# Sums of squares of the first attention: two passes of rounded halves in place of one 32-bit product

## The reference, cut to what matters

```python
def rmsnorm(x, g):
    xf = x.astype(jnp.float32)
    y = xf * lax.rsqrt(jnp.mean(xf * xf, axis=-1, keepdims=True) + EPS)
    return (y * g.astype(jnp.float32)).astype(x.dtype)
...
    k = jnp.concatenate([kv[..., :A_NOPE], jnp.broadcast_to(k_rope[:, :, None, :], (B, L, A_HEADS, A_ROPE))], axis=-1)
    return rmsnorm(k, k_g), kv[..., A_NOPE:]
...
    q = (rmsnorm(h[..., :A_Q_LORA], cq_g) @ w_uq).reshape(B, L, A_HEADS, A_QK)
    return rmsnorm(q, q_g)
```

## Time and profile before

| | |
|---|---|
| median of 3 runs | 3061.49 us (3056.06 to 3071.42) |
| profiled execution, its own time | 3064.81 us |
| span of its instructions | 3063.0 us |
| mean granted TensorE clock | 0.982 of full |
| TensorE busy | 2933.3 us (96%) |
| VectorE busy | 1799.2 us (59%) |
| ScalarE busy | 1360.8 us (44%) |
| GpSimd busy | 701.9 us (23%) |

### The profile page before, as it was taken

The page is one execution under the profiler, slowest core; times in us unless marked ns, Lnnn a source line. Parts: engine busy times, 40 slices in busy tenths (PEclk is TensorE's granted clock), DMA queues, the critical chain, the costliest instruction groups (busy, mean ns, idle before and its releaser), DMA issues. The chain is left out here.

```text
span 3063.0 us, 38159 instructions
## 1 busy us (share of the span) xinstructions
PE 2933.3 (96%) x14042; PEld 2109.6 (69%) x14042; DVE 1799.2 (59%) x2476; ACT 1360.8 (44%) x2162; POOL 701.9 (23%) x509
## 2 busy tenths in 40 slices
PE   5998999999999999999999999979999999999999
PEld 2563444444478888889998887844448788888887
DVE  5124656455535877789863444356643887777442
ACT  3014665656633544445653432136662544445231
POOL 0001555455520133330000000034550133331000
PEclk8998999999999999999999999989999999999999
DMA  9920000000020222224664431122211122224453
GB/s 372 369 98 2 4 3 3 4 2 2 7 110 35 77 83 83 83 83 159 210 196 125 145 102 49 41 66 66 64 45 49 63 78 85 84 85 146 137 171 100
DMA packets 101718, 282.14 MB, mean 92 GB/s; under 512 B 12129, under 2 KB 27745, under 8 KB 94562
## 3 DMA queue, kind: packets, MB, share of 16 engines
q1 hardware_dynamic: 101570, 280.16, 27.4%
HBM read 237.25 MB, written 27.26 MB: 86 GB/s over the span
## 5 line engine op out<-in xcount | busy, mean ns | idle before, releaser
L1367 ACT ACTIVATE z_wh<-part 128x512 fp32r<-128x512 f32 x266 | 166.5, 629 | 335.3 <-PE PS L1238 211.4
L1743 DVE TENSOR_TENSOR z_wdl<-part,z_wdh 128x512 fp32r<-128x512 f32 (+3 forms) x208 | 148.7, 721 | 255.5 <-ACT z_wdh L1420 255.2
L1236 PE MATMUL PS<-s_uh,z_wh 128*128 128x512 f32 x736 | 286.6, 389 | 0.0
L1238 PE MATMUL PS<-s_uh,z_wl 128*128 128x512 f32 x736 | 286.6, 389 | 0.0
L1237 PE MATMUL PS<-s_ul,z_wh 128*128 128x512 f32 x736 | 286.5, 389 | 0.0
L1420 ACT ACTIVATE z_wdh<-part 128x512 fp32r<-128x512 f32 (+3 forms) x208 | 135.2, 655 | 303.7 <-DMA part<-in_w_down 302.7
L1664 DVE TENSOR_TENSOR z_wl<-part,z_wh 128x512 fp32r<-128x512 f32 x266 | 218.2, 833 | 46.3 <-ACT z_wh L1367 46.3
L2400 POOL TENSOR_TENSOR X<-X 128x1024 f32<-128x1024 f32 x96 | 229.4, 2389 | 59.6 <-ACT X L2635 58.7
L1223 POOL TENSOR_TENSOR part<-part,part 128x512 f32<-128x512 f32 x38 | 56.8, 1495 | 777.1 <-DMA part<-in_w_up 777.1
L2635 ACT ACTIVATE X<-PS 128x512 f32<-128x512 f32 x252 | 145.9, 593 | 143.8 <-PE PS L2422 135.5
L2731 DVE TENSOR_REDUCE part<-PS 128x1 f32<-128x512 f32 (+1 forms) x312 | 161.9, 580 | 13.7 <-PE PS L2534 12.9
(11 more groups left out here) (412 smaller groups left out, 7594.6 us busy)
## 6 DMA issues: line engine op xcount, KB each, us to landing
part<-in_w_up SPq DMA_DIRECT2D x132, 512.0 KB, 3.3
part<-in_mod_w SPq DMA_DIRECT2D x48, 1024.0 KB, 7.2
part<-in_w_down SPq DMA_DIRECT2D x96, 256.0 KB, 2.7
gated<-part SPq DMA_DIRECT2D x44, 512.0 KB, 2.6
part<-gated SPq DMA_DIRECT2D x87, 256.0 KB, 5.5
part<-in_w_down SPq DMA_DIRECT2D x32, 384.0 KB, 3.1
part<-in_w_down SPq DMA_DIRECT2D x32, 320.0 KB, 3.2
part<-in_w_down SPq DMA_DIRECT2D x48, 192.0 KB, 2.4
```

What stands on the lines that cost most here:

```text
L1236: pe.matmul(bank_, w_h, x_h, start=start, stop=False, skip_group_check=further)
L1238: return pe.matmul(bank_, w_l, x_h, start=False, stop=stop, skip_group_check=further)
L1367: act.activation(wh[i][:, :], full[b][i], ACT.Copy).then_inc(s["hi"], 1)
L1743: dve.tensor_tensor(wdl[j][:, :width(e)], wd[j][:, :width(e)], wdh[j][:, :width(e)].bitcast(F32), ALU.subtract).then_inc(s["wdl"], 1)
```

## The change

The squares are split: ScalarE copies each square into a rounded high half (`skh` for keys, `sqh` for queries), VectorE subtracts it from the square, which gives the low half (`skl`, `sql`), and TensorE multiplies ones, held in the rounded type as `unity`, by the high half and by the low half, into the same sum in PSUM. The semaphore that `squares` waits for is now that of the subtraction. `square_low` stands in VectorE's queue after `turn` and ahead of the unit step of the chunk before. The shared rows 64 to 96 are split once, at the start. `sq` and `t1` trade their places in memory.

```diff
-            raw, sq = [[Xf[:, rest + (2 * x + n) * BANK:rest + (2 * x + n + 1) * BANK] for n in range(2)] for x in range(2)]
-            t1 = [take(BANK) for _ in range(2)]
+            raw, t1 = [[Xf[:, rest + (2 * x + n) * BANK:rest + (2 * x + n + 1) * BANK] for n in range(2)] for x in range(2)]
+            sql = [place(f"h0_sql{n}", o + n * BANK, BANK) for n in range(2)]
+            sq = [take(BANK) for _ in range(2)]
+            sqh = [place(f"h0_sqh{n}", 9088 + n * BANK, BANK) for n in range(2)]
...
                     def squares(p, w):
 
                         lo, hi = CH[w % 3]
-                        pe.wait_ge(s["sq"], 6 * p + w + 1)
+                        pe.wait_ge(s["sql"], 6 * p + w + 1)
                         if w == 4:
                             pe.wait_ge(s["out"], 6 * p + 4)
                         at_least(pe, "lo", 6 * p + w - 1)
-                        src = sk[0:A_QK, lo:hi] if w < 3 else sq[w % 2][0:A_QK, :hi - lo]
-                        pe.matmul(ps(NB[w % 2], hi - lo, slice(0, A_QK)), ones[0:A_QK, 0:A_QK], src,
-                                  start=True, stop=True).then_inc(s["nt"], 1)
+                        for x in (skh, skl) if w < 3 else (sqh[w % 2], sql[w % 2]):
+                            part = x[0:A_QK, lo:hi] if w < 3 else x[0:A_QK, :hi - lo]
+                            mm = pe.matmul(ps(NB[w % 2], hi - lo, slice(0, A_QK)), unity[0:A_QK, :], part,
+                                           start=x in (skh, sqh[w % 2]), stop=x in (skl, sql[w % 2]))
+                        mm.then_inc(s["nt"], 1)
...
                             act.activation(sk[0:64, lo:hi], ps(PB[w], n, slice(0, 64)), ACT.Square).then_inc(s["sq"], 1)
+                            act.wait_ge(s["sq"], 6 * p + w + 1)
+                            act.activation(skh[0:64, lo:hi], sk[0:64, lo:hi], ACT.Copy).then_inc(s["sqh"], 1)
...
                             act.activation(sq[w % 2][0:96, :n], ps(PB[w], n, slice(0, 96)), ACT.Square)\
                                 .then_inc(s["sq"], 1)
+                            act.wait_ge(s["sq"], 6 * p + w + 1)
+                            act.activation(sqh[w % 2][0:96, :n], sq[w % 2][0:96, :n], ACT.Copy).then_inc(s["sqh"], 1)
...
+                    act.activation(skh[64:96, :], sk[64:96, :], ACT.Copy).then_inc(s["kh0"], 1)
+                    act.activation(unity[:, :], ones[:, 0:A_QK], ACT.Copy).then_inc(s["kh0"], 1)
...
+                    def square_low(p, w):
+                        lo, hi = CH[w % 3]
+                        n = hi - lo
+                        dve.wait_ge(s["sqh"], 6 * p + w + 1)
+                        if w < 3:
+                            out_, in_, h_ = skl[0:64, lo:hi], sk[0:64, lo:hi], skh[0:64, lo:hi]
+                        else:
+                            out_, in_, h_ = [x[w % 2][0:96, :n] for x in (sql, sq, sqh)]
+                        dve.tensor_tensor(out_, in_, h_.bitcast(F32), ALU.subtract).then_inc(s["sql"], 1)
...
                         if kind == "prep" and 3 <= n < 5:
                             turn(p, n)
+                        if kind == "prep" and n < 6:
+                            square_low(p, n)
                         if kind == "prep" and 0 < n < 7:
                             unit(p, b, n - 1)
...
+                    dve.wait_ge(s["kh0"], 1)
+                    dve.tensor_tensor(skl[64:96, :], sk[64:96, :], skh[64:96, :].bitcast(F32), ALU.subtract).then_inc(s["kh0"], 1)
                     for n, x in enumerate((kh[1], kl[1], qh[1], ql[1])):
                         dve.memset(x[96:P, :].bitcast(F32), 0.0).then_inc(s["pad1"], 1)
```

More of the change, by code:

```diff
@@ L2280, in heads0 @@
             osb = take(BANK + P)
+            skh, skl = place("h0_skh", O_MIX + 5 * T, T), place("h0_skl", -(-o // 64) * 64, T)
+            unity = place("h0_unity", 10 * A_HEADS * 64, A_QK)
             rope = ROPE
@@ L2302, in heads0 @@
                      ("one", "one1", "pad", "pad1", "S", "P", "PV", "raw", "rawc",
-                      "sq", "nt", "rt", "ln", "rinv", "t1", "ts", "ta", "out", "hi", "lo", "cast", "vs", "mx", "mc", "mn", "mrow",
+                      "sq", "sqh", "sql", "kh0", "nt", "rt", "ln", "rinv", "t1", "ts", "ta", "out", "hi", "lo", "cast", "vs", "mx", "mc", "mn", "mrow",
                       "mr", "o", "bc", "lnr", "rs", "fin", "ad")}
```

## The result

Over the shared runs the changed kernel took 3117.94 us (4 runs, 3114.99 to 3127.55) against 3061.96 (4 runs, 3056.06 to 3071.42): a ratio of 1.0187 with a 95% interval of 1.0169 to 1.0205. The forecast was 3119. The profiled execution ran 3114.99 us, with a span of 3113.2 and a mean granted clock of 0.975, where before it was 3064.81, 3063.0 and 0.982.

What follows compares the result with a forecast made beforehand. TensorE was taken to set the pace, with late idle waiting for VectorE. Waits of 6.35 less 2.0 saved gave 4.4 us a head, 48 over eleven heads, plus 9 at the first: 57 more, 3119 us, range 3088 to 3140.

Steps and rivals of the forecast that it cites:

- the head period: Head loop: one head goes from 48.6 us to near 53, or 51 if GpSimd never delays the subtractions.
- the hold: Head loop: a subtraction with two SBUF inputs waits for GpSimd's whole addition; 3119 with it, 3095 without, rival's chance 0.20.
- the start: First head, prepared uncovered: TensorE's first product waits behind VectorE's strip fills; 9 us in all, clock included.
- The waits up to w4: Next head's preparation, key chunks w0 to w2, query chunks w3 to w5: added TensorE waits, 2.3 of them at w4.
- the bound of 3.05: Head loop: longest a subtraction beside a GpSimd addition could last, 0.69 + 2.36 = 3.05 us.
- 4.4 - 2.3: Head loop: loss per head as forecast, 4.4 us, less the 2.3 if no subtraction is ever held.
- the sum of the waits: Head loop: added TensorE waits of one head, 1.2 + 1.35 + 0.2 + 0.7 + 2.3 + 0.6 = 6.35 us.
- w5 and the maxima: 0.6 more: End of a head's preparation: TensorE waits 0.6 us more at the last query chunk and the products for the maxima.
- The layout: One head at 490 to 540 us, each instruction placed by its waits; the head before came out at 49.1 us.
- The saving on TensorE: Products of the squares: two cheap passes replace each 32-bit product, saving 2.0 us a head.
- the bound of 0.5 for the changes: TensorE's operand-type changes before 32-bit products: taken as 0, at most 0.09 us at six places, 0.5 a head.
- The clock: Head loop, rival: TensorE's waits lower the clock, losing 1.7 us a head, 19 more, 3138 us; chance 0.09.

Runs made afterwards that it cites:

- The fills: Changed kernel with each GpSimd addition in the head loop replaced by three memsets of about the same total length, softmax sums left out: 3093.26 us, ratio 1.0095.
- Rounded once: Changed kernel without copies and subtractions: ScalarE writes the square rounded, TensorE multiplies it twice, low half left out: 3052.83 us, ratio 0.9970.
- the filled wait: Changed kernel with eight extra TensorE passes ahead of the wait for the halves of w4 (second query chunk): 3118.3 us, ratio 1.0178.
- the run with one pass: Changed kernel without copies and subtractions: square written rounded and multiplied once, low half left out: 3048.6 us, ratio 0.9944.
- subtraction behind the unit step: Changed kernel with each chunk's subtraction moved behind the previous chunk's unit step in VectorE's queue: 3091.44 us, ratio 1.0085.

## Why the prediction was right

The total, the sign, the head period (forecast near 53, measured 53.37), the hold and the start (forecast 9 us) came out as forecast. That the period fits so closely is luck: three terms were off by 0.7 to 2.2 us, and they cancel. That is what can be learned from it.

- **The waits up to w4** came where they were forecast, all of them somewhat shorter. Forecast against measured, in us: w0 1.2 and 1.01; w1 0 and 0; w2 1.35 and 0.73; w3 0.2 and 0; projection of w5 0.7 and 0.50; w4 2.8 and 2.57.
- **The hold** was right, on two rows of another stage. The longest subtractions of that head, 2.22 and 1.65 us, are below the bound of 3.05. The prediction calls the subtraction the only VectorE work of the stage with two SBUF inputs; the two of L603 beside head 11 were overlooked, and they would have shown the hold without going to another stage. The fills show the cause and its worth: 2.29 us a head with the clock, for which the forecast had 4.4 - 2.3 = 2.1. The Trainium skill, "SBUF — State Buffer", section "Who interferes with whom", has the same rule, and the traces agree: with an addition on GpSimd 2.072 us for 256 columns, with a fill 0.418.
- **The term mis-sized most was the sum of the waits**: 6.35 forecast, 5.95 - 1.83 = 4.12 measured (by places: 1.01 + 0.73 + 0.50 + 2.57 - 0.33 at w4, less 0.43 at the maxima, is 4.05). The step that failed is "w5 and the maxima: 0.6 more". The products for the maxima wait 0.53 us a head in place of 0.96, since TensorE, late from w4, finds their inputs nearer to done. A wait that grows early in a head uses up part of a later one. The layout, which placed the kernel before 0.5 us too long, kept both; it also gave w2 0.6 too much.
- **The saving on TensorE** was taken as 2.0 with the changes of operand type at 0. It is 1.29 at full clock, below the 1.5 that the bound of 0.5 for the changes left. The passes of a pair start 0.30 us apart (525.24 to 525.54), not the 0.23 that was to show. Rounded once, the same passes save 1.92. The two kernels differ in their waits: a wait stands ahead of one product a head there (w4) and of five here (all but that of w2), and behind a wait a product overlaps none before it, where otherwise it starts some 0.07 us before the end of that one's record. Whether that is the difference, or the changes of type, no run shows.
- **The clock** is where the ranking failed. It was a rival with a chance of 0.09, and it happened in every head of the loop: 1.92 us of busy time a head against the 1.7 of the earlier trace rows. The rival added its 1.7 to the head's length; there the clock is worth some 1.1, as the heads with the filled wait show. The argument against it was that the waits come apart with TensorE busy between them. Here one wait of 2.57 us is left whole; and even waits that come apart did not always keep the clock up, as the run with one pass shows.
- **The compensation.** Forecast: 6.35 - 2.0 + 0 = 4.4. Measured: 4.12 of idle, 1.29 saved, 1.92 of clock, which is 4.75 against a measured 4.76. The waits were 2.2 too large, the saving 0.7 too large, and the clock 1.9 too small. That these cancel is luck.
- **The start.** The scores were forecast 7.7 us later by layout and 1 more for the clock; 47.0 - 39.3 = 7.7 was measured, the low clock included, so the two terms together were 1 too large. The stage up to the closing copy of head 0 is 104.23 us in place of 91.05. If of these 13.2 us 4.8 are counted as the slower head itself, the start cost 8.4, forecast 9.
- **The sum against the times.** The stage took 915.23 - 250.47 = 664.76 us, against 857.99 - 254.01 = 603.98: 60.8 more, where 57 was forecast and the medians differ by 56. So the median lies nearer to the forecast than the stage does. The rest of the program, 10.6 us shorter in the profiled execution after, is not touched by the change; in the other kernels' profiles, too, the stage begins anywhere from 250 to 260 us. That part is not explained.

As an account of TensorE's time, a head's 4.76 us are: 3.1 of idle from longer chains and queues (the idle without hold, 4.83 and 4.97 with fills and with the subtraction moved, less 1.83), 1.1 of idle from the hold, 1.9 of busy time from the clock, less 1.3 saved. It is an account and not a list of what each repair would return, since a repair of one term changes the others. Half of the intended saving would have been lost in any case, as the kernel with two passes and no subtraction shows.

**What stays open.** What makes the clock fall. Behind a wait of some 2.5 us it fell in ten heads of ten. Behind waits of at most 1.3 us it fell in none (subtraction behind the unit step, 1.2), in six (wait of w4 filled, 1.26) or in three (one pass, 1.1), so the longest wait alone does not decide it. The share of the hold in the clock's fall is not separated either: in the kernel with fills both change together.

## What to carry to other kernels

Work added to an in-order queue is charged at what stands behind it: the subtractions, 3.6 us a head without the hold, went to an engine that was busy 56% of the loop (272.80 of 486.05 us), and the copies to one busy 62% (301.17). With no product waiting for either, they still cost 6 us a head, hold and clock included. Before adding a step, look for the longest wait that stands behind it, find which engine ends it, and put the new work behind the operations that end it; here that gave back 2.9 of 4.8 us, by way of the hold and the clock. When two elementwise engines run side by side, give a VectorE operation with two SBUF inputs a time or a place (an input in PSUM) in which GpSimd's additions can't hold it.

A gain on the busiest engine is worth only what the next chain leaves free: 1.92 us saved on TensorE shortened the head by 0.91, and leaving out one more pass shortened it by 0.25 (47.70 to 47.45) in the heads that kept the clock, and by nothing on the mean.

## What the hardware did that I had not expected

- The granted clock fell in every head of a loop in which TensorE is busy some 89% of the time (474.12 of 533.66 us), during or right behind the longest wait, 2.57 us, and added 1.9 us of busy time a head; in a kernel with 90% (454.86 of 504.51) and 4.97 us of idle a head in pieces of at most 1.2 it did not fall.
- With one pass and waits of at most 1.1 us (TensorE busy 442.59 of 478.65 us), it fell in three heads of ten, behind the same waits as in the other seven.
- The same two passes per chunk saved 1.29 us a head in one arrangement and 1.92 in another, both at full clock; why is not shown.
- Fills that kept GpSimd as busy as the additions (257.87 against 256.45 us in ten heads) did not slow VectorE's subtractions (0.418 and 0.680 us); beside the additions they took 2.072 and 1.112 on the mean.
